# A two-block transformer kernel: gain and gate rows made beside the matmul groups, chained norms from sums of products, residuals folded into the turning

## The reference, cut to what matters

```python
def rms_norm(x, g):                     # over the 2048 columns
    return x * rsqrt(mean(x * x) + 1e-6) * g

# block 1
x = x + concat(attn, conv) @ w_out          # "out1"
h = rms_norm(x, ffn_norm_g)
x = x + conv_glu_ffn(h, w_up, cw, cb, w_down)   # "down1"
x = rms_norm(x, final_norm_g)               # x of block 2
# block 2 (shift, scale, gate come from c, by w_ada)
h = rms_norm(x, g_pre_mix) * (1 + scale_m) + shift_m
o = concat(mla(h), gla(h)) @ w_out_2        # "out2"
x = x + gate_m * rms_norm(o, g_post_mix)
h = rms_norm(x, g_pre_ffn) * (1 + scale_f) + shift_f
f = (silu(h @ w_ffn_gate) * (h @ w_ffn_up)) @ w_ffn_down   # "down2"
return x + gate_f * rms_norm(f, g_post_ffn)
```

## Time and profile before

| | us |
|---|---|
| median of three runs | 2389.18 |
| profiled execution | 2395.41 |
| its span, first to last instruction | 2393.2 |
| TensorE busy | 2285.5 (95%) |
| VectorE busy | 1586.1 (66%) |
| ScalarE busy | 1088.9 (45%) |
| GpSimd busy | 23.3 (1%) |
| mean granted TensorE clock | 0.974 of full |

### The profile page before, as it was taken

How to read it: one execution, slowest core, us unless ns; L and a number is a source line. 1 busy time by engine, 2 the same in 40 slices (tenths; PEclk the granted TensorE clock), 3 DMA queues, 4 the chain that set the end, 5 groups by cost and what they waited for, 6 DMA issues and landing times.

```text
span 2393.2 us, 33537 instructions
## 1 busy us (share of the span) xinstructions
PE 2285.5 (95%) x13738; PEld 2000.4 (84%) x13738; DVE 1586.1 (66%) x2177; ACT 1088.9 (45%) x1605; POOL 23.3 (1%) x59
## 2 busy tenths in 40 slices
PE   7989999999999999999979999988999999999996
PEld 7879877999998899997769776766888988888885
DVE  6896786788887788887664564547555555544444
ACT  5324774544443344444354554445444344444442
POOL 0000000000000000000000000000000000000000
PEclk9989999999999999999989898998999999999998
DMA  8744425588888788888746451345666677655551
GB/s 239 243 140 156 145 89 204 203 278 280 284 300 308 271 289 278 276 281 303 282 126 197 142 177 52 126 143 172 220 232 230 210 236 234 215 185 193 185 194 71
DMA packets 137896, 501.81 MB, mean 210 GB/s; under 512 B 15328, under 2 KB 15456, under 8 KB 137488
## 3 DMA queue, kind: packets, MB, share of 16 engines
q1 hardware_dynamic: 136512, 494.44, 60.6%
q0 software_dynamic: 1232, 5.24, 1.4%
HBM read 494.38 MB, written 5.24 MB: 209 GB/s over the span
## 4 chain that ended last, share of the span: by engine, by line
PE 85%; DVE 9%; ACT 2%; DMA 1%; issue 1%; POOL 1%; SPq 0%; ACTq 0%; DVEq 0%
PE bank L588 53%; PE both L588 26%; DVE w_lo L1527 3%; DVE conv_y L1609 3%; DMA raw<-weights 1%; PE bank L557 1%; ACT w_hi L1089 1%; PE bank L785 1%; PE both L746 1%; PE bank L767 0%; DVE x L2065 0%; DVE wide L2063 0%; PE bank L625 0%; PE bank L1047 0%; PE bank L654 0%
## 5 line engine op out<-in xcount | busy, mean ns | idle before, releaser
L1527 DVE TENSOR_TENSOR w_lo<-raw,w_hi 128x1024 fp32r<-128x1024 f32 x737 | 890.7, 1221 | 519.2 <-ACT w_hi L1089 518.1
L1089 ACT ACTIVATE w_hi<-raw 128x1024 fp32r<-128x1024 f32 x737 | 763.2, 1054 | 672.7 <-PE bank L588 404.0
L588 PE MATMUL bank<-h_hi,w_hi 128*128 128x256 f32 (+1 forms) x2064 | 595.7, 289 | 19.1 <-DVE w_lo L1527 18.4
L588 PE MATMUL bank<-h_lo,w_hi 128*128 128x256 f32 (+1 forms) x2064 | 586.7, 284 | 0.0
L588 PE MATMUL bank<-h_hi,w_lo 128*128 128x256 f32 (+1 forms) x2064 | 586.4, 284 | 0.0
L588 PEld LDWEIGHTS bank<-h_hi,w_hi 128*128 128x128 f32 (+1 forms) x2064 | 397.7, 193 | 29.6 <-DVE w_lo L1527 27.2
L588 PEld LDWEIGHTS bank<-h_lo,w_hi 128*128 128x128 f32 (+1 forms) x2064 | 398.1, 193 | 0.1
L588 PEld LDWEIGHTS bank<-h_hi,w_lo 128*128 128x128 f32 (+1 forms) x2064 | 397.7, 193 | 0.0
L1511 DVE SCALAR_TENSOR_TENSOR ada_acc<-raw,stat,ada_acc 128x1024 f32<-128x1024 f32 x180 | 230.1, 1278 | 0.0
L588 PE MATMUL bank<-w_hi,h_hi 128*128 128x512 f32 (+2 forms) x512 | 190.6, 372 | 0.0
L588 PE MATMUL bank<-w_hi,h_lo 128*128 128x512 f32 (+2 forms) x512 | 190.1, 371 | 0.0
(11 more groups left out here) (329 smaller groups left out, 2732.4 us busy)
## 6 DMA issues: line engine op xcount, KB each, us to landing
raw<-weights SPq DMA_DIRECT2D x924, 512.0 KB, 4.4
bias_rows<-table POOLq DMA_DIRECT2D x1, 3072.0 KB, 35.9
raw<-weights SPq DMA_DIRECT2D x5, 504.0 KB, 3.9
x<-x SPq DMA_DIRECT2D x2, 1024.0 KB, 5.9
bias<-bias_rows POOLq DMA_DIRECT2D x1, 2048.0 KB, 16.9
out<-x SPq DMA_DIRECT2D x8, 256.0 KB, 2.0
phase<-params SPq DMA_DIRECT2D x1, 497.0 KB, 10.5
raw<-weights SPq DMA_DIRECT2D x1, 488.0 KB, 3.5
```

Source lines behind the costliest of these rows:

```text
L588: t = e.matmul(out, s, m, start=opens and first and q == 0, stop=closes and last and q == 2)
L1089: e.activation(w_hi[:, n % PART_SLOTS, 0:widths[i]], raw[:, i % RAW_SLOTS, 0:widths[i]], ACT.Copy).then_inc(hi_ready, 1)
L1527: e.tensor_tensor(w_lo[:, slot, 0:widths[i]], raw[:, i % RAW_SLOTS, 0:widths[i]], w_hi[:, slot, 0:widths[i]].bitcast(F32), ALU.subtract).t ...
```

## The change

Rows of gains and gates are made elsewhere: `down1`, rows 0 and 1 ahead of group 2, row 2 ahead of group 3, row 3 behind the first chunk of group 3; `out2`, rows 0 and 1 behind the first step of group 0, rows 2 and 3 behind its second; `down2`, rows 0 and 1 ahead of group 1, rows 2 and 3 ahead of group 2. They are multiplied in beside later groups, without the factor.

```diff
-                    if half and n == 3:
-                        rows(0, (0, 1, 2))
-                    group(("down1", half, n), 512, pair, ff_hi, ff_lo, ff_need)
-            rows(0, (3,))
+                    if half and n >= 2:
+                        rows(0, ((0, 1), (2,))[n - 2])
+                    down = group_steps(("down1", half, n), 512, pair, ff_hi, ff_lo, ff_need)
+                    next(down)
+                    if half and n == 3:
+                        rows(0, (3,))
+                    whole(down)
...
-                if n == 3:
-                    rows(4, (0, 1, 2))
+                steps = group_steps(("out2", n), 512, pair, mix_hi, mix_lo, mix2_need)
+                if n == 0:
+                    for quarters in ((0, 1), (2, 3)):
+                        next(steps)
+                        rows(4, quarters)
+                whole(steps)
-            rows(4, (3,))
...
-                    if half and n == 3:
-                        rows(8, (0, 1, 2))
+                    if half and n in (1, 2):
+                        rows(8, ((0, 1), (2, 3))[n - 1])
```

```diff
+            def normed(q, dst):
+                w.wait_ge(row_made, q + 1)
+                for tt in range(TT):
+                    if dst is x:
+                        w.wait_ge(row_squares, ...)
+                    e.tensor_tensor(dst[:, tt, cols], x[:, tt, cols], banks[ROW_BANKS[0][q]][:, :], ALU.mult)
...
+                    if half and n == 1:
+                        diagonals(0, param("final_norm_g"), (0, 1))
+                    if half and n == 2:
+                        diagonals(0, param("final_norm_g"), (2, 3))
+                        rests_until(groups[key][11][0] + AHEAD)
+                        normed(0, x)
+                        normed(1, x)
                     if half and n == 3:
-                        diagonals(0, param("final_norm_g"), (0, 1, 2))
+                        rests_until(groups[key][11][0] + AHEAD)
+                        normed(2, x)
+                    residual_group(key, n, x)
+            w.wait_ge(residual, 32)
+            normed(3, wide)
-            add_squares(NORM_FINAL)
-            ... e.scalar_tensor_tensor(x_q, x_q, norm_factors[NORM_FINAL][:, tt:tt + 1], banks[ROW_BANKS[q]][:, :], ALU.mult, ALU.mult)
...
-            add_squares(NORM_MIX2)
-            shift_h(2, norm_factors[NORM_MIX2], 6)
+            t = chain(add_squares(mix2_parts, mix2_totals, 2 * TT, SQUARES_FINAL + 16))
+            w.wait_ge(dve_step, t)
+            chain(e.tensor_scalar(v_mean, mix2_totals[:, 0:TT], 1.0 / D, EPS, ALU.mult, ALU.add))
+            t = chain(e.tensor_scalar(g_mean, mix2_totals[:, TT:], 1.0 / D, None, ALU.mult))
+            w.wait_ge(dve_step, t)
+            e.scalar_tensor_tensor(g_mean, v_mean, EPS, g_mean, ALU.mult, ALU.add).then_inc(square_sums, 1)
+            shift_h(2, scale_mix2)
+            for n in range(3):
+                for tt in range(TT):
+                    x_done = chain(e.tensor_scalar(x[:, tt, cols], x[:, tt, cols], final_factor[:, tt:tt + 1], None, ALU.mult))
```

```diff
+            diagonals(4, ada(2), (0, 1))
             for n in range(4):
-                if n == 3:
-                    rests_until(final["out2", 2] + AHEAD)
-                    diagonals(4, ada(2), (0, 1, 2))
+                if n == 0:
+                    rests_until(groups["out2", 0][3][0] + AHEAD)
+                    diagonals(4, ada(2), (2, 3))
                 rests_until(min(final["out2", n] + AHEAD, gate_first - 1))
+                for tt in range(TT):
+                    if tt:
+                        w.wait_ge(row_squares, SQUARES_O2 + 4 * n + 1)
+                    e.tensor_tensor(wide[:, tt, cols], outs[tt][:, :], gate_row[:, n, :], ALU.mult)
+                for tt in range(TT):
+                    t = chain(e.scalar_tensor_tensor(junk_b[:, :], wide[:, tt, cols], 2.0, x[:, tt, cols], ALU.mult, ALU.mult, accum_out=o2_parts[:, at:at + 1]))
+                    w.wait_ge(dve_step, t)
-            diagonals(4, ada(2), (3,))
-            add_squares(NORM_O2)
-            gated_residual(NORM_O2, 4)
-            add_squares(NORM_FFN2)
+            add_squares(o2_parts, o2_totals, 3 * TT, SQUARES_O2 + 16).then_inc(square_sums, 1)
+            w.wait_ge(row_factors, 5)
+            ... # five 128x2 instructions on u, each waiting for the one before
+            gated_quarter(0, f)
+            shift_h(3, scale_ffn2)
...
+            def gated_quarter(q, factor):       # was: wide = wide * factor * row; x = x + wide
+                for tt in range(TT):
+                    e.scalar_tensor_tensor(x_q, w_q, factor[:, tt:tt + 1], x_q, ALU.mult, ALU.add).then_inc(x_gated, 1)
+            def scale_ffn2(n):                  # inside the turning
+                if n:
+                    gated_quarter(n, o2_factor)
+                w.wait_ge(row_factors, 6)
+                scale_quarter(ffn2_factor, n, x)
```

```diff
+                    if n == 0:
+                        rests_until(groups[key][11][0] + AHEAD)
+                        ... # last ada sums, fold
+                        diagonals(8, ada(5), (0, 1))
+                    if n == 1:
+                        rests_until(groups[key][3][0] + AHEAD)
+                        diagonals(8, ada(5), (2, 3))
+                    if n:
+                        rests_until(groups[key][11][0] + AHEAD)
+                        gate_rows(n - 1)
                     residual_group(key, n, wide)
-            diagonals(8, ada(5), (3,))
-            add_squares(NORM_F2)
-            gated_residual(NORM_F2, 8)
+            add_squares(f2_parts, f2_total, TT, SQUARES_F2 + 8).then_inc(square_sums, 1)
+            gate_rows(3)
+            for q in range(4):
+                gated_quarter(q, f2_factor)
```

More of the change, by code:

```diff
@@ L654, in rows @@
                     e.matmul(banks[b][:, :], ones, diag[:, q % 2, :], start=True, stop=True).then_inc(row_made, 1)
+                    free[b] = rows_used(first, q)
             w.wait_ge(gains_landed, 16)
@@ L1073, in tensor_program @@
                     else:
[L1074 to L1075 removed]
+                        free[pair[0]], free[pair[1]] = (o_copied, 4 + 2 * n + 1), (o_copied, 4 + 2 * n + 2)
         def scalar_program(e):
@@ L1261, in scalar_program @@
                     if half:
[L1262 to L1268, removed]
+                        for which in (("x0",), ("x1",), ("g0", "g1", "x2"), ("g2", "x3", "g3"))[n]:
+                            square_final(which)
             w.wait_ge(folded, 1)
@@ L1547, in rest_h, with add_squares, scale_quarter @@
-            def rest_h(stage, gain, factors, count):
-                scale_h(factors, count, (0, 1))
+            def add_squares(parts, totals, groups_of, count):
+                w.wait_ge(row_squares, count)
+                return e.tensor_reduce(totals, parts.rearrange("p (g n) -> p g n", g=groups_of), AX.X, ALU.add)
+            def scale_quarter(factors, n, src):
+                cols = slice(n * 512, (n + 1) * 512)
+                for tt in range(TT):
+                    e.tensor_scalar(wide[:, tt, cols], src[:, tt, cols], factors[:, tt:tt + 1], None, ALU.mult).then_inc(scaled, 1)
@@ new lines, in vector_program @@
+            w.wait_ge(row_factors, 5)
+            f, u = o2_factor, ffn2_mean
+            t = chain(e.tensor_tensor(u, o2_totals[:, 2 * TT:], f, ALU.mult))
+            w.wait_ge(dve_step, t)
+            t = chain(e.tensor_tensor(u, u, o2_totals[:, TT:2 * TT], ALU.add))
+            w.wait_ge(dve_step, t)
+            t = chain(e.tensor_tensor(u, u, f, ALU.mult))
+            w.wait_ge(dve_step, t)
+            t = chain(e.tensor_tensor(u, u, x_squares, ALU.add))
+            w.wait_ge(dve_step, t)
@@ L2103, in vector_program @@
                 for n in range(4):
+                    key = ("down2", half, n)
                     if half == 0:
-                        rests_until(final["down2", 0, n] + AHEAD)
+                        rests_until(final[key] + AHEAD)
                         continue
-                    if n == 3:
-                        rests_until(final["down2", 1, 2] + AHEAD)
+                    if n == 0:
+                        rests_until(groups[key][11][0] + AHEAD)
                         add_ada_before(len(widths))
```

194 lines of the change are left out of this document (116 added, 78 removed).

## The result

| | before | after |
|---|---|---|
| median of the timed runs, us | 2390.86 (2389.16 to 2395.10) | 2367.22 (2362.81 to 2368.66) |
| profiled execution / its span, us | 2395.41 / 2393.2 | 2368.23 / 2366.4 |
| mean granted clock | 0.974 | 0.978 |

Ratio 0.9901, 95% interval 0.9889 to 0.9913: 23.6 us faster. Forecast: 2368.4.

What follows compares the result with a forecast made beforehand. TensorE, busy 95% of the span, was taken as the bound, so only its standstills could be won. Gains of 10.1 (`down1`), 3.3 (`out2`), 7.4 (`down2`) and 0 (`out_attn`), 20.8 us, off 2389.18 gave 2368.4; range 2361.5 to 2377.

Steps and rivals of the forecast that it cites:

- Price of a row: Wherever rows are made: each costs TensorE some 1.12 us with its pauses, four rows 4.5 us.
- `down1`, tail: From the end of `down1`'s last group to the next matmul: 8.6 us in place of 18.33, gain 9.7.
- `c_kv`: Scalings of x and two small steps on VectorE ahead of the rests of `c_kv`: 0.5 us lost, bounds 0 and 2.8.
- `out2`, inside: Inside `out2`'s groups: new 3.4 us wait for a diagonal behind the second step, 0.8 for the clock; loss 3.6 us.
- `out2`, tail: Behind `out2`, up to the first matmul: 11.85 us instead of 19.08, gain 7.2.
- C: Rival: the fused gated add takes double, 1.3 us; 7.8 us lost, 2376.2 us; chance 0.04.
- Turning: Behind `out2`: quarters 2 and 3 are gated inside the turning, 1.35 us each; 0.3 us lost.
- End: Tail of `down2` to the end of the kernel: 12.0 us for 17.04, gain 5.0.
- A: Rival: the wait in `out2` does not come; 25.0 us gained, 2364.2 us; chance 0.11.
- B: Rival: GpSimd's powers cost by the column, `out2`'s stop brings the full half-clock price; 16.2 us gained, 2373.0; chance 0.15.
- D: Rival: half of the two middle tails' gain, 8.5 us, is lost in the next stretch; 2376.9 us; chance 0.05.
- E: Rival: 28.7 us of VectorE work in the groups is not hidden, 2397.1; decided by its 8 us lag; chance 0.03.

Runs made afterwards that it cites:

- e3: Kernel after, with the six scalings of x laid one behind each of the first six rests of `c_kv`: 2360.32 us, ratio 0.9877.
- e6: Kernel before, with only the rows and diagonals of `down1` and `down2` made early: 2377.04 us, ratio 0.9940.
- e1: Kernel after, with VectorE turning to the `out2` rows one chunk earlier: 2358.16 us, ratio 0.9864.
- e2: Kernel after, with TensorE's second pair of `out2` rows two steps later, VectorE's order untouched: 2358.41 us, ratio 0.9862.
- e4: Kernel after, with VectorE's first gated adds behind `out2` held until GpSimd has made the second factor: 2365.93 us, ratio 0.9896.
- e7: Kernel after, with the second norm behind `out2` taken from squares of x after all four quarters are gated: 2365.53 us, ratio 0.9898.
- e5: Kernel after, with 12 or 20 idle products of 0.72 us added on VectorE in group 2 of `down1`: 2374.90 and 2373.30 us (one each).
- the control: Kernel after run once more, nothing edited: 2365.93 us, ratio 0.9888.
- e8: Kernel after, with the edits of e1 and e3 together: 2359.89 us, ratio 0.9863.

## Why the prediction was right

By its own steps, in the order of the sum:
- **Price of a row.** Taken as 1.12 us, measured 0.86: a pair of rows adds 1.72 us to its stretch, the slower first matmul behind it included, alike at the pair and the two single rows in `down1` and at both pairs in `down2`. The 1.12 came from three rows behind a wait of 1.9 us. This one term, too high by 0.26, is four times 0.26 = 1.04 us at each of the two seams, and that is what both inside gains were too small by: 1.86 for 0.9 and 3.45 for 2.4.
- **`down1`, tail.** 9.7 said, 9.67 measured. The power over four columns was taken at 0.95 with bounds of 0.55 and 2.2; it took 1.03.
- **`c_kv`.** The 0.5 us was measured (0.6), and its reason is wrong: e3 took the scalings away from there and got 0.12 back, and e6, which has none, took as long as the kernel after (26.86 and 26.87). The loss is 1.3 us more of half clock at `c_q`'s start. The number is right by luck; the term is 0.
- **`out2`, inside.** The wait came where and as it was derived, 3.25 us for 3.4, and e1 and e2 took it away; 0.23 us more came ahead of rows 0 and 1, which the forecast put at nothing. The loss was 1.8 instead of 3.6. Four cheaper rows are 1.0 of that. The fall of the clock went the other way, 1.6 us where 0.8 was said. It was outweighed on the other side: before itself ran the first 4.7 us of `out2` at half clock and the kernel after began it at full clock, which the forecast missed. So these two terms cancel in part by luck. Under an equal clock the loss is 1.8 as well, without either: e6, with the code of before, and the second execution of the kernel after both began `out2` with 2 us of half clock and had no more, and to the last matmul on the weights they took 93.5 and 95.3. That is the 3.6 without the 0.8 for the clock and with the cheaper rows. The forecast put a fall behind the stop of 2.4 us and none behind 1.9; the length does not tell them apart: windows from 1116 to 1120 us of before have a granted clock of 0.60, behind a wait of 1.85 us.
- **`out2`, tail.** 6.8 for 7.2. GpSimd's second factor was put at 1.05 us with its hand-overs and took 1.89 beside the gated adds (e4): the first scaling stood at +7.3 us and not at +6.9, which is the 0.4 missing. The gated add itself took 0.67 us, as read off its longer kin; so C, at double, falls.
- **Turning.** 0.3 said, 0.36 measured, and again for another reason. From the first matmul of `gate` to the last transpose took 21.27 us before, 21.63 in the kernel after and 21.31 in its second execution; half clock at the start of this lasted 3.6, 4.3 and 3.7 us. Half of that taken off, it is 19.5 us in all three, and the timelines of TensorE show no wait there that before has not. e7, which gates everything ahead of it, has 19.5 too (20.95 less half of 2.9). Gating inside the turning cost nothing.
- **End.** 5.3 for 5.0, six gated adds in 3.98 us: chain of the kernel after,
```profile
2358.41 0.75 DVE x L2130
...
2359.83 3.98 DVE x L2130 x6
```
- **Not in the sum:** 2.7 us in stretches for which nothing was forecast. 1.9 of them lie between `c_kv` and `out2`, where before ran at half clock for 36 us and the kernel after for 31; the difference lies where `c_q` is turned.

Of the rivals, A is refuted for this kernel: the wait came in both its profiled executions. B is refuted in its first half by the 1.03 us for four columns and 0.70 for two; of its dearer fall of the clock, 2.4 us instead of 0.8, half came (1.6). D and E didn't come. E's point of decision holds nearly: the lead on VectorE is 8.5 us, of which one block can take 7.3 (e5), and the longest new block is 2.7. Beyond 7.3 each us would have cost a us.

That the median fell on the forecast within 1.2 us is partly luck: the gain between the medians is 23.6 us where 20.8 was said, and the median of before that the forecast started from, 2389.18, is 1.7 below that of four runs, which took back more than half of the difference. The kernel's own executions spread over 7 us by the clock, which is more than this.

Open: what decides whether the clock comes back after 3 or after 16 us. All four executions of e3 lay at the low level and one of four of the control; e8, with the same edit, was at both. So an effect of that edit on the clock is neither shown nor excluded.

## What to carry to other kernels

Follow a wait backwards through slots: a diagonal behind a rest, a rest behind a rounding, a rounding behind TensorE's leaving the slot is a wait that can be computed from the code to 0.2 us, and moving either end by one or two chunks takes it away. Reckon what an engine's lead covers with the work that already stands in it: of 8.5 us, a rest of 1.2 and products of 2.4 left 4.8. Compare edits worth under 5 us by the stretch that holds them, cut at the same matmul in both traces, and only then by medians. Take work off a serial tail first (9.7, 6.8 and 5.3 us here): it was gained whole.

## What was not expected of the hardware

- The granted clock after one and the same wait differs between executions of one kernel: 3 or 16 us at 1.2 GHz after 0.8 us of standing still, none, 3.4 or 6.8 us after 3.25. It is worth 1.6 to 5 us a place, as much as most edits here.
- GpSimd's two steps of a norm's factor take 0.19 and 0.70 us alone and 0.61 and 1.09 beside VectorE's gated adds.
- A power on GpSimd costs 0.55 us for one column, 0.70 for two and 1.03 for four (rows of GpSimd and of the chain above): some 0.16 for each further column.
